# Making the last quarter of a cross-attention output projection in products of 128 moving columns instead of 256

## What is computed

```python
x = x + (concat([a_out, b_out]) @ w_out)                      # mixing block
h = rms_norm(x, norm_xattn_g);  m = rms_norm(mem, norm_mem_g)
q, k, v = h @ wq, m @ wk, m @ wv
o = softmax(q k^T / 16) v                                     # 4 heads of 256
x = x + o @ wo                                                # the product changed here: 1024 x 1024 x 1024
h = rms_norm(x, norm_ffn_g)
x = x + moe_ffn(h, router_w, router_b, w_up, b_up, w_down, b_down)
return rms_norm(x, final_norm_g)
```

## Time and profile before

| | us |
|---|---|
| median of 3 runs | 2784.63 (2783.31 to 2787.39) |
| the profiled execution | 2790.99 |
| its span (first to last instruction) | 2789.2 |
| output projection, first to last matmul start | 937.4 to 1029.5 |
| its last chunk | 1006.5 to 1029.6 |

### The profile page before, as it was taken

How to read it: one execution, slowest core, us unless ns; L and a number is a source line. 1 busy time by engine, 2 the same in 40 slices (tenths; PEclk the granted TensorE clock), 3 DMA queues, 4 the chain that set the end, 5 groups by cost and what they waited for, 6 DMA issues and landing times.

```text
span 2789.2 us, 35993 instructions
## 1 busy us (share of the span) xinstructions
PE 2539.9 (91%) x12228; PEld 2069.4 (74%) x12295; DVE 1901.7 (68%) x1971; ACT 1277.8 (46%) x1355; POOL 369.7 (13%) x310
## 2 busy tenths in 40 slices
PE   4999888879897998679999999999999999999994
PEld 3889676859784796467777877777777777777773
DVE  4399693851404327778897777768877778898776
ACT  3211433230314221356675655556555566676554
POOL 0000000001000012111121221212221221221111
PEclk8999866759899996789999999999999999999997
DMA  3111200211010010898998878779878788999777
GB/s 116 48 59 46 76 31 9 68 61 39 31 46 16 1 46 38 299 306 293 321 364 275 283 251 297 244 237 304 290 247 298 250 283 292 333 364 323 249 248 250
DMA packets 267447, 531.82 MB, mean 191 GB/s; under 512 B 10940, under 2 KB 45040, under 8 KB 267280
## 3 DMA queue, kind: packets, MB, share of 16 engines
q1 hardware_dynamic: 249952, 474.51, 48.2%
q0 software_dynamic: 15232, 53.49, 8.2%
q10 hardware_dynamic: 2192, 2.81, 0.4%
HBM read 491.19 MB, written 39.58 MB: 190 GB/s over the span
## 4 chain that ended last, share of the span: by engine, by line
PE 77%; DVE 13%; issue 4%; ACT 4%; DMA 1%; DVEq 1%; ACTq 0%; POOL 0%; POOLq 0%; SPq 0%
PE PS L2057 12%; PE PS L2059 11%; PE PS L2058 11%; PE PS L1725 8%; PE PS L2065 6%; PE PS L2062 6%; PE PS L1882 3%; PE PS L1948 3%; DVE wlo L1523 2%; PE PS L2027 1%; PE PS L1935 1%; DVE Ssc L1201 1%; PE PS L1900 1%; ACT whi L838 1%; PE PS L1765 1%
## 5 line engine op out<-in xcount | busy, mean ns | idle before, releaser
L1523 DVE TENSOR_TENSOR wlo<-raw,whi 128x2048 fp32r<-128x2048 f32 x395 | 897.4, 2288 | 200.4 <-ACT whi L838 182.7
L838 ACT CAST whi<-raw 128x2048 fp32r<-128x2048 f32 x395 | 746.0, 1911 | 181.3 <-PE PS L2065 136.2
L2057 PE MATMUL PS<-whi,xhi 128*128 128x512 f32 x1056 | 439.9, 417 | 41.0 <-DVE yb L1606 18.5
L2059 PE MATMUL PS<-whi,xlo 128*128 128x512 f32 x1056 | 415.0, 393 | 0.0
L2058 PE MATMUL PS<-wlo,xhi 128*128 128x512 f32 x1056 | 413.3, 391 | 0.0
L2059 PEld LDWEIGHTS PS<-whi,xlo 128*128 128x128 f32 x1056 | 199.5, 189 | 44.0
L2057 PEld LDWEIGHTS PS<-whi,xhi 128*128 128x128 f32 x1056 | 201.0, 190 | 41.2 <-DVE wlo L1523 6.5
L2058 PEld LDWEIGHTS PS<-wlo,xhi 128*128 128x128 f32 x1056 | 200.1, 189 | 40.2
L2057 PE MATMUL PS<-whi,hhi 128*128 128x512 f32 x512 | 202.6, 396 | 0.0
L2059 PE MATMUL PS<-whi,hlo 128*128 128x512 f32 x512 | 199.7, 390 | 0.0
L2058 PE MATMUL PS<-wlo,hhi 128*128 128x512 f32 x512 | 199.4, 389 | 0.0
(11 more groups left out here) (368 smaller groups left out, 4754.3 us busy)
## 6 DMA issues: line engine op xcount, KB each, us to landing
raw<-in_exp_w_up SPq DMA_DIRECT2D x267, 1024.0 KB
raw<-in_exp_w_down SPq DMA_DIRECT2D x128, 1024.0 KB
ring<-in_w_in SPq DMA_DIRECT2D x11, 1024.0 KB, 5.3
xres<-in_x SPq DMA_DIRECT2D x4, 1024.0 KB, 12.9
ring<-in_xattn_wk SPq DMA_DIRECT2D x4, 1024.0 KB, 7.6
ring<-in_xattn_wv SPq DMA_DIRECT2D x4, 1024.0 KB, 4.9
ring<-in_w_out SPq DMA_DIRECT2D x4, 1024.0 KB, 5.0
xres<-in_x SPq DMA_DIRECT2D x1, 4096.0 KB, 13.4
```

What stands on the lines that cost most here:

```text
L838: nc.scalar.copy(whi[:, chunk_slot(c, NSPL), :], raw[chunk_slot(c, NRAW)][:]).then_inc(s_whi, 1)
L1523: nc.vector.tensor_tensor(wlo[:, chunk_slot(c, NSPL), :], raw[chunk_slot(c, NRAW)][:], whi[:, chunk_slot(c, NSPL), :].bitcast(F), ALU.subtract
L2057: pe.matmul(o, hi[:, k, :], wh, start=first and bias is None, stop=False)
L2059: ins = pe.matmul(o, lo[:, k, :], wh, start=False, stop=stop and kk == 3)
```

## The change

The projection's chunks 0 to 2 stay. In chunk 3 each token tile is made in two groups, `m = 2t` and `2t + 1`, of 128 moving columns. Group `m` has PSUM bank `m % 8`, of which it uses 128 columns; each group is again 24 matmuls, each with its own weight load, and the two groups of a tile load the same stationary pieces. Each group raises o_product by itself, so that the semaphore ends at 40 and not at 32, and the three waits for all of it (POOL, ACT, DVE) are set to 40. DVE adds each group by itself, 128x128, and raises o_drained once per tile, after the second add. PE's wait ahead of a group is for the last reader of its bank: the tile of chunk 2 for the first eight groups, and tile `t - 4` of chunk 3 for the others.

```diff
@@ DVE, add_residual
                         n = TT * c + t
+                        if seg == "o" and c == 3:
+                            for m in (2 * t, 2 * t + 1):
+                                dve.wait_ge(s_mm[seg], n - t + m + 1)
+                                xs = xres[:, t, 256 * c + P * (m % 2):256 * c + P * (m % 2 + 1)]
+                                ins = nc.vector.tensor_tensor(xs, xs, PS[:, m % 8, 0:P], ALU.add)
+                            ins.then_inc(s_dr[seg], 1)
+                            continue
                         dve.wait_ge(s_mm[seg], n + 1)
@@ PE, output projection
             for c in range(4):
                 pe.wait_ge(s_dlv, 4 + c + 1)
+                if c == 3:
+                    break
                 for t in range(TT):
...
+            for m in range(2 * TT):
+                t, cols = m // 2, slice(P * (m % 2), P * (m % 2 + 1))
+                pe.wait_ge(s_dr["o"], 2 * TT + m + 1 if m < 8 else 3 * TT + t - 3)
+                tile = slice(P * t, P * (t + 1))
+                for k in range(KT):
+                    for i, (a, b) in enumerate(((oxH, woH), (oxH, woL), (oxL, woH))):
+                        ins = pe.matmul(PS[:, m % 8, 0:P], a[:, k, tile], b[1][:, k, cols],
+                                        start=(k == 0 and i == 0), stop=(k == KT - 1 and i == 2))
+                ins.then_inc(s_mm["o"], 1)
@@ POOL, ACT, DVE: the waits for the whole product
-            pool.wait_ge(s_mm["o"], 32)
+            pool.wait_ge(s_mm["o"], 40)
-            act.wait_ge(s_mm["o"], 32)
+            act.wait_ge(s_mm["o"], 40)
-                    dve.wait_ge(s_mm["o"], 32)
+                    dve.wait_ge(s_mm["o"], 40)
```

## The result

| | before | changed | forecast |
|---|---|---|---|
| median of 10 runs each, side by side (us) | 2786.48 | 2798.75 | 2806.0 (2801 to 2850) |
| ratio of the two, with 95% interval | | 1.004 [1.0028, 1.0052] | 1.0077 |
| profiled execution (us) | 2790.99 | 2799.12 | 2812.4 |
| its span (us) | 2789.2 | 2797.3 | |
| last chunk, PE busy (us) | 23.10 | 43.00 | 44.5 |

The change makes the kernel slower by 12.3 us (8 to 15). I had forecast 21.4. The chunk itself did cost almost what was predicted, and some 7 us came back later, in a place that the sum had set to nothing.

What follows compares the result with a forecast made beforehand. TensorE alone was taken to bound the output projection, so its extra time reaches the end whole: 21.50 - 0.13 = +21.4 us on the median 2784.63 gives 2806.0 us, range 2801 to 2850.

Steps and rivals of the forecast that it cites:

- Part 1: Chunk 3 of the output projection: 384 matmuls 0.116 us apart instead of 192 at 0.120, +21.5 us, all on the path.
- Part 2: TensorE's waits for a free bank in chunk 3: met long before, cost nothing.
- Part 3: VectorE's adds in chunk 3: sixteen of about 0.29 us, +1.3 us hidden; only the last add counts, -0.13 us.
- Part 4: Waits for 40 and the stages after the projection: nothing new late, 0, with +-1.5 us for a later start.
- The sum on the median: Whole kernel: profiled execution lay 6.4 us over the median; the same difference kept on the median gives 2806.0 us.
- A: Chunk 3's matmul price follows the columns, 0.067 us between starts, +2.5 us, 2787.2 us; chance 0.08.
- B: Chunk 3's float32r matmuls below 256 columns run as four passes, 0.227 us apart, +64.1 us, 2848.6 us; chance 0.13.
- D: Chunk 3: the change doesn't do what it says, through a TensorE wait between groups; no size or own chance given.
- C: TensorE's clock drops to 1.2 GHz within chunk 3, 0.213 us a matmul, up to +58.8 us, 2838 to 2843; chance 0.05.
- The sustained figure of about 81 ns: Skill's rule set against the sum: 384 matmuls of chunk 3 would take 31.1 us, +8.1 us.
- Slower at 0.91: Whole kernel: chance 0.91 of being slower by more than 0.2%, or 5.6 us.
- the load's floor: Chunk 3: 0.107 us per matmul for the weight load alone, +18.0 us; gave the range's low end, 2801.

Runs made afterwards that it cites:

- twice256: The changed kernel, but each of the last chunk's 384 matmuls moves 256 columns instead of 128; 2799.25 us, ratio 1.004 to the kernel before.
- half128: The kernel before, but the last chunk's 192 matmuls move 128 columns instead of 256, the other half not made; 2800.95 us, ratio 1.0046.
- cols64: The changed kernel, but with the last chunk in 32 groups of 64 columns, 768 matmuls; 2912.27 us, ratio 1.0452 to the kernel before.
- before_pad128: The kernel before with 64 tiny bf16 matmuls (128 instructions) ahead of TensorE's first work; 2779.77 us, ratio 0.9972.
- delay: The kernel before with sixteen extra VectorE adds of 128x1024 between the last residual add and the norm; 2799.77 us, ratio 1.0044.
- after_again: The changed kernel, unaltered, run once more for a second profile; 2801.8 us, ratio 1.0049 to the kernel before.
- before_again: The kernel before, unaltered, run once more for a second profile; 2786.13 us, ratio 0.9996.

## Why the prediction was right and wrong

**Part 1, the matmuls: right, at the edge of its range.** Predicted 0.116 us between starts, +21.5 us, range 0.112 to 0.120. Measured 0.1115 us and 384 x 0.1115 - 23.04 = +19.8 us. Of the two rows between which I took the middle, the one with the right number of columns (plain float32, 0.112) was the right one, and the middle put 1.7 us too much on the chunk. At 256 columns the 0.120 us of the earlier trace rows is not the load plus something but the columns' own 0.107 plus 0.013. The better reading of my own rows was a maximum of two: the load, 0.107 by the clock and 0.111 by the earlier trace rows, or the columns by the line through the earlier trace rows. twice256, half128 and cols64 fit it.

**Part 2, waits on PE: right.** PE and PEld busy 43.00 and 42.98 of 43.00 us.

**Part 3, the adds: right.** 0.29 us each, hidden but for the last.

**Part 4, the waits for 40 and what follows: the step that failed.** It said "0, with +-1.5 us for what the later stages make of another start". In the router that held (19.5 us behind after 19.6). But the change adds 384 instructions to PE's stream, and the step never looked at the code's place. That term measured -7.8 us (-11.4 to -4.5), as before_pad128 has it alone. With it the sum would have been 19.8 - 0.1 - 7.8 = +11.9 against the measured 12.3; that this agrees to less than a us is more than the interval of the term promises. It was also wrong to keep the clock's part at 1.5 us: twice256 and delay each moved some 4 us ahead of the loop, about half of it by the clock and the rest in its train.

**The sum on the median.** The profiled execution lay 6.4 us over the median. I carried that over as a constant, which was sound for the medians, but it hid that the profiled execution has a wait of 5 us in its loop that others don't have.

**The rivals.** A (by columns, 0.067 us) and B (four passes, 0.227 us) are excluded by the starts, D by the stretch without a gap. C, the clock, didn't come at 128 columns; cols64 shows it one halving further on. The sustained figure of about 81 ns at 128 columns, in the Trainium skill's "TensorE: Matmul & The Clock Gate", section "Back-to-back issue gap", would have given a chunk of 31.1 us; the trace has 43.0, so for float32r the measurement decides against it.

**Slower at 0.91** was right: the ratio's interval, 1.0028 to 1.0052, lies wholly above 0.2%. The range failed at its low end, since all of its width went upwards to rivals about the price, and nothing below the load's floor was thought of that wasn't a price. A term of either sign for the rest of the kernel, as wide as its own executions differ (2783 to 2790.99 us in what was shown of before), would have held the time.

## What to carry to other kernels

A float32r matmul with its own weight load costs the larger of two, a fixed 0.111 us (the load, as I read it) or the columns' time, so fewer than 256 columns on a stationary piece only add loads; at 64 columns the granted clock fell as well, and the price of a matmul went from 0.112 to 0.213 us. A change in the number of an engine's instructions ahead of a loop moves the loop's code, and that alone was worth some 8 us here (4.5 to 11.4), two fifths of what the change itself costs; before believing a difference of 0.3%, put filler ahead until both kernels lie at the same place, and compare them there. Sixty-four idle matmuls in the first wait (before_pad128) made a version 0.28% faster than the kernel before (0.16 to 0.41%), and so faster than both kernels. That holds for this loop; its place was not chosen by a rule but found.

## What the runs showed that I had not expected

**PE waits for its code.** The count of instructions and the packets inside the waits say so: up to 10.1 us in one wait (after_again), and only in the first passes of the loop: after 1242 us no wait of PE reaches 2 us in any kernel of the table. The period of 256 instructions agrees with the block in the Trainium skill's "Runtime: NRT & Kernel Launch", section "Instruction fetch mechanics": kernels shifted by 256 show the waits of those that aren't. The same section of the Trainium skill says that crossing a block is mostly hidden, and that a taken branch out of the window has to fetch first. The waits of 2.8 to 10.1 us by "issue", in a loop that branches, are on the side of the second sentence; no run here takes the branches out.

**VectorE beside GpSimd.** The scaled row of the norm (128x1024) takes 1.2 us each in the group of three ahead of the router, and 4.4 us where GpSimd's add of 32x2048 has started before it, in before_again:

```profile
1032.61 3.68 DVE L1385 SCALAR_TENSOR_TENSOR h<-xres,st,gfb 128x1024 f32<-128x1024 f32 x3
...
1041.61 4.44 DVE L1385 SCALAR_TENSOR_TENSOR h<-xres,st,gfb 128x1024 f32<-128x1024 f32 x1
```

```profile
1040.91 9.06 POOL L485 TENSOR_TENSOR bstage<-bstage,bup 32x2048 f32<-32x2048 f32 x2
```

**The router paid back the longer chunk.** twice256 starts its last add 3.5 us later than the changed kernel, its router's first add 1.6 us later and its second 0.7 us earlier. The first step goes with the clock, which was at 1.00 for 10.2 us (the sixteen matmuls above took 1.87 us and not 3.46). The second follows from it and is the pair of the paragraph above: the scaled row between the two adds started at 1063.22 us, ahead of GpSimd's add (1064.46), and took 2.23 us; in the changed kernel GpSimd's add starts first, and the row takes 4.51. When the clock rises there is not known; no run here tried it by itself.
